# The combine of a mixture-of-experts layer: norm tables loaded behind the expert rows, gate tables ahead of them as before

## What is computed

```python
mw = (moe_router[l], moe_router_bias[l], moe_w_gate[l], moe_w_up[l], moe_w_down[l], ...)
xp = _layernorm(ALPHA * xp + mp[5] * _moe(_modulate(xp, mp[3], mp[4]), *mw), ln2_g[l], ln2_b[l])
xs = _layernorm(ALPHA * xs + ms[5] * _moe(_modulate(xs, ms[3], ms[4]), *mw), ln2_g[l], ln2_b[l])
# in _moe: 64 experts, 8 per token
y = out[dest] * w.reshape(-1)[order][:, None]
return jax.ops.segment_sum(y, tok, num_segments=n)   # + the shared expert
```

## Time and profile before

| | us |
|---|---|
| Median of three timed runs | 1741.38 |
| The profiled execution's own time | 1748.69 |
| Its span, first to last instruction | 1746.8 |
| TensorE busy | 1548.8 (89%) |
| VectorE busy | 597.9 (34%) |
| ScalarE busy | 356.1 (20%) |
| GpSimd busy | 260.7 (15%) |
| Moved by DMA | 586.76 MB, mean 336 GB/s |

### The profile page before, as it was taken

One profiled execution on the slowest core, in us unless ns is written; L12 is line 12 of the kernel. 1 busy time (PEld: TensorE's weight loads), 2 busy tenths in 40 slices (PEclk: granted clock), 3 DMA queues, 4 the chain that ended last, 5 costly groups with the idle time before them and its releaser, 6 DMA issues. The chain is left out here.

```text
span 1746.8 us, 19238 instructions
## 1 busy us (share of the span) xinstructions
PE 1548.8 (89%) x6878; PEld 744.8 (43%) x6878; DVE 597.9 (34%) x1424; ACT 356.1 (20%) x770; POOL 260.7 (15%) x229
## 2 busy tenths in 40 slices
PE   4899889897799899999887989898699989899887
PEld 1566644542344344344335744533243434344333
DVE  3233685532123111111148773632133111111117
ACT  3224621111111111111114272211011111111120
POOL 0010121111011123111104100111111122211100
PEclk9999999999899999999998989999899999999999
DMA  9890388599999999999994015689999999999994
GB/s 383 343 359 27 135 340 348 214 418 421 392 412 420 410 375 412 395 416 418 368 404 151 12 45 225 268 343 421 412 383 421 411 397 376 402 409 411 390 366 184
DMA packets 112499, 586.76 MB, mean 336 GB/s; under 512 B 22154, under 2 KB 24618, under 8 KB 54160
## 3 DMA queue, kind: packets, MB, share of 16 engines
q1 hardware_dynamic: 89264, 533.84, 75.5%
q0 software_dynamic: 22560, 50.00, 7.5%
q10 hardware_dynamic: 576, 1.66, 0.3%
HBM read 570.99 MB, written 45.30 MB: 353 GB/s over the span
## 5 line engine op out<-in xcount | busy, mean ns | idle before, releaser
L2990 DVE TENSOR_TENSOR scratch<-scratch,bank 128x256 f32<-128x256 f32 x84 | 51.5, 613 | 584.8 <-ACT scratch L2958 556.3
L2865 PE MATMUL bank<-weights,scratch 128*64 128x512 f32 x384 | 183.0, 631 | 45.8 <-DMA scratch<-in_moe_w_up 41.6
L2865 PE MATMUL bank<-scratch 128*64 128x512 f32 x352 | 168.0, 632 | 37.9 <-DMA weights<-in_moe_w_up 24.8
L2866 PE MATMUL bank<-scratch 128*64 128x512 f32 x384 | 186.6, 642 | 0.0
L2866 PE MATMUL bank<-weights,scratch 128*64 128x512 f32 x384 | 181.8, 627 | 0.0
L2958 ACT ACTIVATE scratch<-bank 128x256 f32<-128x256 f32 x84 | 32.2, 383 | 644.0 <-PE bank L2866 424.8
L2865 PEld LDWEIGHTS bank<-weights,scratch 128*64 128x64 f32 x384 | 53.8, 145 | 161.6 <-issue 161.3
L2865 PEld LDWEIGHTS bank<-scratch 128*64 128x64 f32 x352 | 49.6, 145 | 144.3 <-issue 144.1
L2595 POOL DMA_INDIRECT y_rows<-hP,y_idx x39 | 41.5, 1063 | 448.4 <-ACT hP L2966 330.5
L2580 POOL DMA_INDIRECT hP<-h_rows,tok_idx x78 | 81.3, 1043 | 135.4 <-PE bank L2541 61.7
L2871 PE MATMUL bank<-weights,scratch 128*128 128x512 f32 x224 | 98.6, 593 | 2.7 <-DMA weights<-in_moe_w_up 2.7
(11 more groups left out here) (400 smaller groups left out, 2445.9 us busy)
## 6 DMA issues: line engine op xcount, KB each, us to landing
weights<-in_moe_w_gate SPq DMA_DIRECT2D x62, 1024.0 KB, 12.8
weights<-in_moe_w_up SPq DMA_DIRECT2D x62, 1024.0 KB, 20.1
weights<-in_moe_w_down SPq DMA_DIRECT2D x62, 1024.0 KB, 21.3
scratch<-in_moe_w_gate SPq DMA_DIRECT2D x60, 1024.0 KB, 12.6
scratch<-in_moe_w_up SPq DMA_DIRECT2D x60, 1024.0 KB, 21.8
scratch<-in_moe_w_down SPq DMA_DIRECT2D x60, 1024.0 KB, 21.4
weights<-in_w_mod SPq DMA_DIRECT2D x6, 2048.0 KB, 11.4
wmod_more<-in_w_mod SPq DMA_DIRECT2D x6, 2048.0 KB, 8.6
```

Source lines behind the costliest of these rows:

```text
L2865: nc.tensor.matmul(out[0:HALF, :], x[:, 0:HALF], w0[:, kk], start=(kk == 0), stop=(kk == KT - 1))
L2866: m = nc.tensor.matmul(out[HALF:P, :], x[:, HALF:P], w1[:, kk], start=(kk == 0), stop=(kk == KT - 1))
L2990: nc.vector.tensor_tensor(B.h[b % 2].rearrange("p (j q) -> p q j", j=2), B.ex[b % 2].rearrange("p (q j) -> p q j", j=2), k.ps[2 + b % 2][: ...
```

## The change

`combine_tables` is split. `combine_gates` stands where it stood and loads only the two gate tables, on the same semaphore. `combine_norm_tables` loads the norm's tables, on a new semaphore `s_tables`, and stands on SyncE behind the last group of expert rows. `centred(0)` on VectorE waits for all of them: two in layer 1, four in layer 0.

```diff
--- before.py
+++ after.py
@@ -1815,22 +1815,27 @@
             eng.dma_start(M.T[:, cnd, 1 + j, :], k.fold1_d[cnd, j:j + 1, :].to_broadcast([P, D])).then_inc(s_tab, 16)
 
 
-def combine_tables(k, eng, layer):
+def combine_gates(k, eng, layer):
 
     M = NormBuffers(k, 2)
+    for cnd in range(2):
+        k.load_ahead(eng, 4, M.T[:, cnd, 0, :], k.mod_d[layer, cnd:cnd + 1, 5 * D:6 * D].to_broadcast([P, D]))
+
+
+def combine_norm_tables(k, eng, layer, s_tables):
+
+    M = NormBuffers(k, 2)
 
     def load(out, row):
-        eng.dma_start(out, row.to_broadcast([P, D])).then_inc(k.s_ahead[4], 16)
-        k.ahead[4] += 16
-
-    for cnd in range(2):
-        load(M.T[:, cnd, 0, :], k.mod_d[layer, cnd:cnd + 1, 5 * D:6 * D])
-        if layer + 1 < DEPTH:
-            for j in range(2):
-                load(M.T[:, cnd, 1 + j, :], k.fold_d[cnd, j:j + 1, :])
+        eng.dma_start(out, row.to_broadcast([P, D])).then_inc(s_tables, 16)
+
     if layer + 1 == DEPTH:
         for j, n in enumerate("gb"):
             load(M.gb[:, j, :], k.io[f"ln2_{n}"][layer:layer + 1, :])
+        return
+    for cnd in range(2):
+        for j in (1, 0):
+            load(M.T[:, cnd, 1 + j, :], k.fold_d[cnd, j:j + 1, :])
 
 
 class FoldRows:
@@ -2794,7 +2799,7 @@
         for i, e in waiting:
             down(i, e)
         sp.wait_ge(s_d, places.z_done + 1)
-        combine_tables(k, sp, layer)
+        combine_gates(k, sp, layer)
 
     def on_gpsimd(pool):
         last_tok, last_row = bounds(pool)
@@ -3204,6 +3209,7 @@
     s_acc, s_d, s_v, s_p, s_nb, s_h, s_tr, s_out = sems(
         nc, ctx, "cb_row_added cb_steps cb_var cb_rstd cb_shift cb_h cb_turned outputs_stored")
     s_mu, s_sq = sems(nc, ctx, "cb_mean cb_squares")
+    s_tables = sems(nc, ctx, "cb_tables_loaded")[0]
     squares = k.s[:, 1440:1440 + D]
     assert n_diag * P <= 1440
     s_g = k.pool_sems[layer][5:11]
@@ -3218,6 +3224,7 @@
                 sp.wait_ge(sem, blocks)
                 a = h * half + n * rows
                 sp.dma_start(v.rearrange("p (j n) -> p j n", j=rows), src[:, a:a + rows, :]).then_inc(s_g[i], 16)
+        combine_norm_tables(k, sp, layer, s_tables)
         if last:
             for t in range(TILES):
                 sp.wait_ge(s_h, t + 1)
@@ -3310,6 +3317,8 @@
 
         def centred(t):
             G = M.gb[:, 0, :] if last else M.T[:, min(t, 1), 2, :]
+            if t == 0:
+                dve.wait_ge(s_tables, 16 * (2 if last else 4))
             if t < SUMMED_BY_ACT:
                 dve.wait_ge(s_mu, t + 1)
             st.mark(nc.vector.scalar_tensor_tensor(k.cat[:, t, :], k.x[:, t, :], M.mv[:, t, 0:1], G,
```

## The result

| us | before | after |
|---|---|---|
| Median | 1742.84 (8 runs, 1738.28 to 1751.06) | 1748.51 (8 runs, 1747.62 to 1750.27) |
| The profiled execution's own time | 1748.69 | 1748.25 |
| Its span | 1746.8 | 1745.9 |

The ratio of after to before is 1.0029, 95% interval 1.0016 to 1.0042. The changed kernel is slower by 5.1 us (2.8 to 7.3); 1750.2 was forecast. The two profiled executions don't show it in their spans (the one of before lies 6 us above its median), so the difference has to be read inside the two combines.

A forecast was written before the change was run, and what follows sets the result against it. Bound by the combine's row-transfer landings, then VectorE's work. Costs 4.2 + 3.4 + 0.8 + 0.4 = +8.8 us on the 1741.38 median gave 1750.2 us; range 1744.0 to 1754.5, leaving out two in ten.

The forecast's parts named there:

- likeliest case: Both combines: the tables' late landing outweighs the earlier rows; +8.8 us, to 1750.2 us; chance 0.62.
- Part 1: Combine's row transfers: with fewer tables ahead, rows land 5.6 us earlier in layer 0, 3.4 in layer 1.
- rival C: Row transfers: landings don't depend on what stood ahead, tables land behind the old last rows; 1759.2 us; chance 0.06.
- Part 2: VectorE at `centred(0)`: it waits for tables landing behind the rows; +4.2 us in layer 0, +3.4 in layer 1.
- Rival B: Tables at `centred(0)`: they land in time, the wait is free and earlier rows pay; 1734.2 us; chance 0.06.
- late engine: Row and table transfers: one or a few of 16 DMA engines lag and set landings; 4.8 to 4.9 us per 2 MB.
- Part 3: TensorE's closing products, third tile: idleness lowers its clock; +0.8 us in layer 0, +0.4 in layer 1.
- The sum: Both combines: 4.2 + 3.4 for the tables' wait and 0.8 + 0.4 for TensorE's clock, +8.8 us.
- Rival A: DMA in unprofiled runs: little lateness, layer 1 costs 0 to 1, layer 0 4.2 to 8; 1746.4 to 1749.5; chance 0.26.
- The signs: Profile after: idle before `centred(0)` 9 to 10 us (layer 0), 5 to 7 (layer 1); earlier row additions; clock falls.
- the theory: Combine's DMA: rows and tables pass a late engine in issue order, so tables behind rows wait for those in front.

The follow-up runs named there:

- form before: Kernels whose combine, in the layer counted, has all tables issued ahead of the expert rows; a class of kernels, with no single time.
- form after: Kernels whose combine, in the layer counted, has the norm tables issued behind expert rows; a class of kernels, with no single time.
- shorter filler: Changed kernel plus 7 (layer 0) and 4 (layer 1) useless TensorE products before the third tile's closing products; ratio to the kernel before 1.0037.
- layer 0 alone: Changed kernel, but layer 1 keeps its norm tables ahead of the rows; against the kernel before, ratio 1.0044, +7.7 us.
- layer 1 alone: Changed kernel, but layer 0 keeps its norm tables ahead of the rows; against the kernel before, ratio 1.0022, +3.8 us.

## Why the prediction was right

The forecast was that of the likeliest case, and it holds by its mechanism: rows earlier, tables where the last rows used to land, a wait that outweighs the gain. The time itself came nearer than the working deserves. The cost was forecast at 8.8 us and measured at 5.1; 1750.2 is only 1.7 us off 1748.51, partly because the median of before is 1742.84 over its eight runs, 1.5 above that of the three runs that the prediction started from. The profiles can be laid side by side by counting from the first row issue. Each number is a mean, with the executions it comes from; those that were told singly stand above.

| us from the first row issue | form before | form after | difference | predicted |
|---|---|---|---|---|
| fourth group of rows, VectorE's last wait for rows, layer 0 | 31.9 (3) | 25.6 (10) | -6.3 | -5.6 |
| the same, layer 1 | 30.3 (2) | 27.2 (10) | -3.1 | -3.4 |
| `centred(0)`, layer 0 | 37.7 (3) | 41.2 (5) | +3.5 | +4.2 |
| the same, layer 1 | 36.1 (2) | 39.2 (5) | +3.1 | +3.4 |
| last `scaled(2)`, layer 0 | 56.8 (3) | 61.3 (3) | +4.4 | +5.0 |
| the same, layer 1 | 54.6 (2) | 58.6 (3) | +4.0 | +3.8 |

(The ten are the kernels with nothing but the gate tables ahead in that layer and norm tables somewhere behind; the five those with all of them behind group 6; the three those of the five without filler.)

*Part 1, rows earlier.* Right in both layers, so rival C falls: the rows' landings do depend on what stood ahead of them. For a table ahead of the rows that is 1.6 us in both (6.3 / 4 and 3.1 / 2), where 1.4 and 1.7 stood in the prediction; behind the rows one costs 1.2. In layer 1 the mean of before rests on two executions 2.5 us apart (31.5 and 29.1), so 1.6 is uncertain there by some tenths.

*Part 2, the tables behind the rows.* Right. Rival B, tables there in time, needed a landing before `centred(0)` asks; more than nine and more than six microseconds of wait, in every execution of this form, rule it out. The landing itself can be compared: before, the last rows landed 41.8 us after the first row issue in layer 0 and 40.1 in layer 1, and `centred(0)` starts with the last table at 41.2 and 39.2 now. The prediction had them equal in layer 0 and the table 0.6 us earlier in layer 1; rival C had 45.9 and 44.1. The wait can now be built up from the last group that VectorE reads: two more groups at 4.9 us and two tables at 1.24, less the 5.73 us that VectorE has to do until `centred(0)` (1709.38 to 1715.11), make 6.55 in layer 1, measured 6.63. With four tables and 5.72 us it is 9.04 in layer 0, measured 9.46. The rule of the Trainium skill that the prediction weighed (DMA: Bandwidth & Descriptors, "Anatomy of one DMA"), a transfer's time without a late engine, would have made layer 1 free. The trace doesn't agree, as the wait there is 6.6 us; the page states the rule as a fit for transfers that GpSimd issues, and these are issued by SyncE. The Trainium skill has a sentence that fits what the earlier place did (DMA: Bandwidth & Descriptors, "Queues, rings and completion order"): each engine consumes the descriptors of its ring in order. The trace agrees: a group of 2 MB less in front, 4.6 and 4.9 us less to wait.

*Part 3, the clock.* The mechanism was right, the size in layer 1 was not: VectorE waits 0.85 and 0.97 us for the slower products, where 0.8 and 0.4 stood in the sum. The prediction had TensorE idle for some 5 us in layer 1 and 9.6 in layer 0; it was 6.76 and 7.34, and the closing products are about as slow behind either. That these waits are the clock's is shown by the shorter filler that took 0.57 and 0.97 off them.

*The sum* was +8.8; the last rows of the table give +8.4. The timed difference is 5.1 (2.8 to 7.3) and 7.8 (5.2 to 10.4), so +8.8 is high for the first measurement and inside the second. Part of the 8.4 comes from which executions were profiled. The rows are issued once the last scatter has landed, and that comes 8.5 to 9.6 us ahead of the MEMSET on VectorE, the end of the experts, in some executions and 12 to 14 in others, of either form. In layer 0 one of the three before is of the first kind, and none of the three after. Without that one, the last `scaled(2)` there goes from 57.9 to 61.3 us after the first row issue: +3.4 and not +4.4. Counted from the MEMSET the means are 45.6 before and 48.7 after in layer 0, 43.1 and 46.7 in layer 1, so +3.1 and +3.6; that count errs the other way, as the rows were issued 11.2 us ahead of it in the mean of the three before and 12.6 in that of the three after. Over all ten kernels of the form after it is 11.2 as well, so this is chance and no gain of the change. The profiles thus give some 7 us, uncertain by a microsecond or more with two or three executions to a mean, which both timed measurements allow.

*Rival A*, little lateness when nothing is profiled, is not refuted outright: a trace exists only of profiled executions, and the total can't tell, since its 5.0 to 8 us cover both measurements, and layer 0 alone, 7.7, suits it too. Two measurements speak against it. It gave layer 1 a cost of 0 to 1, and layer 1 alone costs 3.8, though the interval (1.0 to 6.4) just touches that. And tables one group earlier save 10.4 us on one chip (1.0045 to 0.9985, by the intervals some 4 us either way at most), where rival A leaves a group of 4.9 in layer 0 and at most 1 in layer 1. The prediction also set the Trainium skill's line on two slower engines (DMA: Bandwidth & Descriptors, "Latency and other measured facts") against rival A; the page says it of traces and ties it, as a guess, to the descriptor rings of GpSimd's transfers, so it is no evidence for runs without a profile.

*The signs.* The waits at `centred(0)` lie in the ranges given (9 to 10 and 5 to 7 us). The tail of landings by a late engine in layer 1 isn't gone, but it is shorter. From the fall of the DMA share to the last landing it is 8 to 10 us in the two executions of the form before and 4 to 6 in those of the form after. By the theory that is as it should be, since the tables behind the rows lengthen the other engines' work behind the first row issue and the late engine had a backlog anyway. Two readings in the prediction are a little off and change nothing: the tables are issued some 8 us ahead of the rows (8.0 and 8.3), not 9, and the next layer's weights 13.6 us after the last rows, not 10.

## What to carry to other kernels

A small load that is moved off the front of a burst does make the burst land earlier, but behind the burst it lands when the burst's last byte used to; whether that is a gain is decided by where its first reader stands among the readers of the burst. Put it right behind the last part that stands ahead of its reader: here behind group 4 of 6, which turned +0.3 to +0.45% into -0.3 to -0.4%. And read landings where a reader was seen to wait, not from the mean rate: the pace is the same (2.1 MB / 416 GB/s = 5.0 us, and 4.9 between landings), but the engine that is last stood some 10 us behind the others in the kernel before and 4 in the changed one.

## What the runs showed that was not expected

- The wait at `centred(0)` repeats across executions and chips far better than the times do: 9.46, 9.44, 9.40, 9.39 and 9.75 us in layer 0, 6.63, 6.65, 6.66, 6.66 and 6.63 in layer 1, in kernels with all norm tables behind the rows, while times of one kernel spread over up to 16 us. If VectorE's last rows and the tables land by the same late engine, its lateness cancels in the wait; that it is the same engine no run here shows.
- The issue of the first rows falls into two groups against the end of the experts (8.5 to 9.6 and 12 to 14.2 us ahead of it), in either form. What decides between them, no run here shows.
- TensorE's clock can fall behind a short idle stretch too: its closing products took 2.53 us behind 2.37 us of idleness, though it had worked without a pause for 30 us up to then. Behind 1.46 us or less they took 1.88 to 1.98.
